# Third modulation in the second mixer, dense layer zero in two phases, and the convolution's first tap on ScalarE

## What is computed

```python
def swiglu(h, wg, wu, wd):
    return (jax.nn.silu(h @ wg) * (h @ wu)) @ wd

def second_block(x, c, ada_w, ada_b, ...):
    cs = jax.nn.silu(c)
    for i in range(2):
        mod = cs @ ada_w[i] + ada_b[i]
        sh1, sc1, g1, sh2, sc2, g2 = [m[:, None, :] for m in jnp.split(mod, 6, axis=-1)]
        h = rms_norm(x, norm_mix_g[i]) * (1 + sc1) + sh1
        if i % 2 == 0:
            mix = hybrid_mixer_2(h, hy_w_in[0], ..., hy_w_out[0], rel_table)
        else:
            mix = conformer_conv(h, cv_w_pw1[0], ..., cv_w_pw2[0], cv_b_pw2[0])
        x = x + g1 * mix
        h = rms_norm(x, norm_ffn_g[i]) * (1 + sc2) + sh2
        x = x + g2 * swiglu(h, ffn_w_gate[i], ffn_w_up[i], ffn_w_down[i])
    return rms_norm(x, final_norm_g)
```

## Time and profile before

| | us |
|---|---|
| median of 3 runs (lowest, highest) | 1461.85 (1460.13, 1463.21) |
| the profiled execution | 1465.13 |
| its span | 1463.4 |
| TensorE busy | 1376.3 (94%) |
| VectorE busy | 870.7 (60%) |
| ScalarE busy | 275.6 (19%) |
| GpSimd busy | 265.6 (18%) |
| mean granted clock | 0.976 |
| DMA | 355.58 MB, 243 GB/s |

### The profile page before, as it was taken

How to read it: one execution, slowest core, us unless ns; L and a number is a source line. 1 busy time by engine, 2 the same in 40 slices (tenths; PEclk the granted TensorE clock), 3 DMA queues, 4 the chain that set the end, 5 groups by cost and what they waited for, 6 DMA issues and landing times. The chain is left out here.

```text
span 1463.4 us, 18944 instructions
## 1 busy us (share of the span) xinstructions
PE 1376.3 (94%) x7517; PEld 1015.5 (69%) x7517; DVE 870.7 (60%) x1464; ACT 275.6 (19%) x602; POOL 265.6 (18%) x342
## 2 busy tenths in 40 slices
PE   5999999896776999999999999999999999999997
PEld 1877655653442788768888888777766878888843
DVE  2458775432232668753454685788783874777864
ACT  2222221000000311643345101000002113211101
POOL 5078010000000300553355402100020100000000
PEclk9999999998888999999999999999999999999999
DMA  9976887899999697866774455898854552555431
GB/s 350 310 263 226 285 329 298 348 417 415 416 418 385 191 305 261 306 194 162 159 180 133 160 162 176 327 333 322 297 210 150 155 156 73 163 168 172 170 129 47
DMA packets 176057, 355.58 MB, mean 243 GB/s; under 512 B 7289, under 2 KB 137041, under 8 KB 158561
## 3 DMA queue, kind: packets, MB, share of 16 engines
q1 hardware_dynamic: 166720, 313.64, 60.4%
q0 software_dynamic: 9248, 40.71, 9.5%
HBM read 352.58 MB, written 1.74 MB: 242 GB/s over the span
## 5 line engine op out<-in xcount | busy, mean ns | idle before, releaser
L1846 PE MATMUL PS<-HT,ring 128*128 128x256 f32 x1152 | 258.3, 382 | 0.1
L1846 PEld LDWEIGHTS PS<-HT,ring 128*128 128x128 f32 x1152 | 215.5, 190 | 36.0 <-issue 7.9
L1542 DVE TENSOR_TENSOR X<-X,PS 128x1024 f32<-128x1024 f32 x14 | 17.1, 1222 | 113.2 <-PE PS L1318 113.2
L1265 PE MATMUL PS<-ring_extra,slot_rows 128*32 128x256 f32 x576 | 56.3, 450 | 27.6 <-DMA ring_extra<-in_expert_w_gate 7.1
L2876 PE MATMUL PS<-HT,ring 128*128 128x256 f32 x352 | 76.8, 379 | 0.0
L2905 PE MATMUL PS<-ada_stage,half_sums 128*128 128x256 f32 x320 | 75.6, 379 | 0.0
L2905 PE MATMUL PS<-ring,half_sums 128*128 128x256 f32 x320 | 75.6, 379 | 0.0
L2876 PEld LDWEIGHTS PS<-HT,ring 128*128 128x128 f32 x352 | 66.7, 190 | 9.0
L2882 PE MATMUL PS<-ring,hid 128*128 128x512 f32 x160 | 71.8, 592 | 0.0
L2905 PE MATMUL PS<-ring,HT 128*128 128x256 f32 x304 | 68.8, 379 | 0.0
L2905 PEld LDWEIGHTS PS<-ring,half_sums 128*128 128x128 f32 x320 | 59.4, 190 | 11.2 <-issue 4.3
(11 more groups left out here) (736 smaller groups left out, 2465.4 us busy)
## 6 DMA issues: line engine op xcount, KB each, us to landing
ring<-in_hy_w_in SPq DMA_DIRECT2D x40, 1024.0 KB, 8.4
ring_extra<-in_w_ada SPq DMA_DIRECT2D x24, 1024.0 KB, 7.9
ada_stage<-in_ada_w POOLq DMA_DIRECT2D x24, 1024.0 KB, 7.3
ring<-in_ffn_w_gate SPq DMA_DIRECT2D x22, 1024.0 KB, 5.9
ring<-in_ffn_w_up SPq DMA_DIRECT2D x22, 1024.0 KB, 5.8
ring<-in_ffn_w_down SPq DMA_DIRECT2D x22, 1024.0 KB, 5.8
ring_extra<-in_expert_w_down SPq DMA_DIRECT2D x18, 1024.0 KB, 22.9
ring_extra<-in_expert_w_up SPq DMA_DIRECT2D x18, 1024.0 KB, 20.1
```

The lines of the kernel that those rows point to most:

```text
L1265: mm = pe.matmul(PS[e * SLOTS:(e + 1) * SLOTS, 2, j * CW:(j + 1) * CW], hs[:, k, e * SLOTS:(e + 1) * SLOTS], w[e][:, k, :], start=(k == 0) ...
L1542: dve.tensor_tensor(part, part, PS[:, 6:8, :], ALU.add).then_inc(added, 1)
L1846: mm = pe.matmul(dst, w[:, k, half * P:(half + 1) * P], HT[:, k, :], start=(k == 0), stop=(k == KT - 1))
```

## The change

1. Dense layer zero takes the form of dense layer one (`SPLIT_ORDER` for both, the functions get the layer f). The weight sums of its first chunk are made by VectorE in the second mixer, between `combine_a(1)` and `combine_b(1)`.
2. The third modulation moves into the second mixer. Its 24 fetches go on SyncE's queue, between the ring's loads, into two buffers in turn (a region of the convolution's and the second modulation's stage); a fetch waits until the add two before it is done. The 24 adds stand at `THIRD_ADDS` on VectorE. TensorE sums at (25, 0), (31, 0) and (36, 3) (4, 2 and 2 matmuls of 512 columns, each after 8, 16, 24 adds) and turns at (25, 2), (31, 2) and (37, 1); ScalarE copies between; VectorE finishes at (25, 3), (31, 3) and (37, 1). `value(m)` waits for the first finish (m < 4) or the second, the output projection for the third. Bias rows are small loads now, added by small operations.
3. At the end of dense layer zero the row sums and columns go; `gate_rows` moves between the two halves of the norm's turning.
4. ScalarE does the first tap of the mixer's convolution (24 operations), VectorE the other three.
5. The second modulation's adds come a step earlier, and the value sums are spread anew.
6. Buffers: `third_acc` is carried from the mixer to the end, other slabs are cut anew, and GpSimd makes `tap_blocks` and loads the second gate's bias only once dense layer zero is done.

```diff
-        add_at = {(s, 3): s - 2 for s in range(2, 18)}
+        ADD_PLACES = [(s, 3) for s in range(1, 14)] + [(14, 2), (15, 1), (16, 0)]
+        add_at = {at: a for a, at in enumerate(ADD_PLACES)}
+        THIRD_ADDS = ((20, 2), (21, 1), (21, 2), (22, 0), (22, 2), (23, 1), (24, 0), (24, 3), (25, 2), (26, 1), (27, 0), (27, 3),
+                      (28, 2), (29, 1), (30, 0), (30, 3), (31, 2), (32, 1), (33, 0), (33, 3), (34, 2), (35, 1), (35, 3), (36, 2))
...
-        v_sum_at = {(14, 3): (0, 0), (15, 1): (0, 1), (15, 2): (0, 2), (15, 3): (0, 3),
-                    (16, 1): (1, 0), (17, 2): (1, 1), (17, 3): (1, 2), (18, 1): (1, 3)}
+        v_sum_at = {(14, 3): (0, 0), (15, 3): (0, 1), (16, 1): (0, 2), (16, 2): (0, 3),
+                    (17, 0): (1, 0), (17, 3): (1, 1), (18, 0): (1, 2), (18, 2): (1, 3)}
...
+                def fetch_third(a):
+                    if a == 0:
+                        sp.wait_ge(used, base + V0 + 3)
+                    elif a == 1:
+                        sp.wait_ge(cols, 1)
+                    else:
+                        sp.wait_ge(third_summed, a - 1)
+                    sp.dma_start(third_stage[a % 2].rearrange("p (a n) -> p a n", a=1), wv3[:, ds(a % KT, 1), a // KT, :])\
+                        .then_inc(third_in[a % 2], 16)
...
                 for s in range(NP + 12):
+                    for a in range(THIRD):
+                        if (THIRD_ADDS[a - 2] if a > 1 else ((19, 1), (20, 1))[a]) in ((s, 0), (s, 1)):
+                            fetch_third(a)
...
                     send_until(sp, base + s + 1)
+                    for a in range(2, THIRD):
+                        if THIRD_ADDS[a - 2] in ((s, 2), (s, 3)):
+                            fetch_third(a)
...
+                    pe.wait_ge(third_made, 2 if m >= 4 else 1)
...
+                def sum_third(c):
+                    pe.wait_ge(third_summed, THIRD_READY[c])
...
+                    for g in range(2 * len(THIRD_PARTS[c])):
+                        v = third_acc[:, THIRD_PARTS[c][g // 2], :].rearrange("p (m h k) -> p h k m", h=2, k=KT // 2)[:, g % 2]
+                        mm = pe.matmul(PS[32 * g:32 * g + 32, 7, :], ones[:, 0:32], v, start=True, stop=True,
+                                       tile_position=(0, 32 * g))
+                    mm.then_inc(third_rowsum, 1)
...
+                def tap(s):
...
+                    act.wait_ge(evac, s + 1)
+                    for m in range(2):
+                        tile = 2 * XORDER[s] + m
+                        act.activation(conv_tiles(s)[:, m, :], RX[:, s % 3, m, 0:S], ACT.Identity, scale=convT[:, tile:tile + 1],
+                                       bias=convT[:, CONV * XT + tile:CONV * XT + tile + 1]).then_inc(first_tap, 1)
...
+                def add_third(a):
+                    g, k = a // KT, a % KT
+                    dve.wait_ge(third_in[a % 2], 16 * (a // 2 + 1))
+                    dst = third_acc[:, THIRD_AT[g]:THIRD_AT[g] + 2, :].rearrange("p a n -> p (a n)")
+                    if k == 0:
+                        dve.tensor_scalar(dst, third_stage[a % 2], cv[:, 0:1], None, ALU.mult).then_inc(third_summed, 1)
+                    else:
+                        dve.wait_ge(third_summed, a)
+                        dve.scalar_tensor_tensor(out=dst, in0=third_stage[a % 2], scalar=cv[:, k:k + 1], in1=dst,
+                                                 op0=ALU.mult, op1=ALU.add).then_inc(third_summed, 1)
...
                 combine_a(1)
+                first_gate, first_up = (segs["ffn0"].base + j for j in range(2))
+                for n in (first_gate, first_up):
+                    dve.wait_ge(landed[slots[n]], 16 * turns[n])
...
                 combine_b(1)
...
     def chunk(f, kind, e):
-        return FFN_BASE[f] + (order, SPLIT_ORDER)[f].index((kind, e))
+        return FFN_BASE[f] + SPLIT_ORDER.index((kind, e))
```

More of the change, by code:

```diff
@@ L2929, in seven @@
                 hs7 = lambda j: [hsum[:, j, k, :] for k in range(4)]
-                ws7 = lambda j: [wsum[:, e % 2, j, k, :] for k in range(4)]
-                arrive(pe, n_g)
-                arrive(pe, n_u)
-                pe.wait_ge(combined, weights_summed(f, e))
-                if e > 1:
-                    pe.wait_ge(combined, row_sum(f, e - 1, 2))
-                product(P2, rows(1, 0), half(gate, 1))
-                product(P1, rows(0, 0), half(gate, 0)).then_inc(used, 1)
-                if e > 1:
-                    pe.wait_ge(combined, row_sum(f, e - 1, 5))
@@ L3007, in split_gate_up @@
-            def split_gate_up(e, norm):
-                n_g, n_u = chunk(1, "g", e), chunk(1, "u", e)
-                gate, up = w_slot(n_g), w_slot(n_u)
-                half = lambda ap, h: [ap[:, 4 * h + k, :] for k in range(4)]
-                rows = lambda h, i: [HT[:, 4 * h + k, i * P:(i + 1) * P] for k in range(4)]
-                hs7 = lambda j: [hsum[:, j, k, :] for k in range(4)]
-                ws7 = lambda j: [wsum[:, (e + 1) % 2, j, k, :] for k in range(4)]
+                ws7 = lambda j: [wsum[(e + 1) % 2][:, j, k, :] for k in range(4)]
@@ L3128, in _ @@
             turn(0)
-            ffn(0, 0, turn_vectors, modulation_rows)
-            modulation_columns()
-            gate_rows(1, 0, 0)
-            pe.wait_ge(gated, 4)
-            turn(1)
+            for e in range(FFN_CHUNKS):
+                split_gate_up(0, e, 0)
+                if e == 0:
+                    turn_vectors()
+            for gi in range(len(DOWN_GROUPS)):
+                split_down(0, gi)
+            whole_down(0)
+            turn_row(1, 0)
+            gate_rows(GATE_MIX, 0)
+            turn_row(1, 1)
             for f in range(KT):
@@ L3412, in split_sum_weights @@
-            def split_sum_weights(e):
-                for n in (chunk(1, "g", e), chunk(1, "u", e)):
-                    dve.wait_ge(landed[slots[n]], 16 * turns[n])
-                if e >= 2:
-                    dve.wait_ge(sevens, PE_MARKS[1, e - 2, "P4"])
-                gate, up = w_slot(chunk(1, "g", e)), w_slot(chunk(1, "u", e))
-                t1, t2, t4 = (wsum[:, (e + 1) % 2, j] for j in range(3))
-                step(dve.tensor_tensor(t1, up[:, 0:4, :], gate[:, 0:4, :], ALU.subtract))
-                step(dve.tensor_tensor(t2, up[:, 4:8, :], t1, ALU.subtract))
-                step(dve.tensor_tensor(up[:, 0:4, :], up[:, 4:8, :], up[:, 0:4, :], ALU.subtract))
-                dve.tensor_tensor(t4, gate[:, 4:8, :], t2, ALU.subtract).then_inc(combined, 1)
```

678 lines of the change are left out of this document (249 added, 429 removed).

## The result

The changed kernel takes 1503.55 us (median of 4 runs, 1503.2 to 1504.75) where the kernel before takes 1461.51 (4 runs): a ratio of 1.0287, with a 95% interval of 1.0272 to 1.0302. It is **42 us slower**. The forecast was slower by 5 us, with 1477 as the upper end of the range. The direction was right; the size was not, and neither were most of the places.

The account below looks back on a forecast made before the run. TensorE was taken to bound the second mixer and dense layer zero. Dense side -11.3, sums and turns +6.3, waits +10.6 gave +5.6, taken as +5.2: 1467 us as a median, range 1456 to 1477.

Parts of the forecast that it names:

- What I cost at nothing: Priced at zero: first tap on ScalarE, 24 fetches on SP's queue, GpSimd's later tap blocks and bias load.
- steps 20 to 23: Mixer, before the first score: five adds delay `move_y(15)`, a TensorE wait of 0.5 to 4 us, taken as 2.2.
- the value stage: Value products, steps 14 to 18: waits vanish or grow with tighter fetches, -1.3 to +2.5 us, taken as +0.5.
- ahead of the first pointwise product: From dense layer zero's end to the first pointwise product: 7.0 us instead of 5.0, a loss of 1.9.
- The gain in dense layer zero: Dense layer zero takes dense layer one's form: 207.6 us instead of 220.8, -13.2, its weight sums hidden on VectorE.
- Sums and turns on TensorE: Mixer: three third-modulation sums (5.0 us) and three turns (1.3) add 6.3 us, bounds 5.3 to 7.3.
- Waits for adds in the attention: TensorE waits for VectorE's adds: 3.0, 2.2 and 1.0 us at the three sums, 1.0 and 0.7 at `value`.
- the 3.09 us each, from which 1470 was worked out: Attention: adds contending with GpSimd take 3.09 us instead of 2.35, four waits grow 0.74 each: 1470 instead of 1467.
- rival 4: TensorE's clock falls after waits of about 3 us, each fall costing 2 to 3 us: 1469 to 1473; chance 0.05.
- Rival 1: VectorE is in time at sums (25,0), (31,0) and their values, so waits vanish: 1456.9 or 1455.5; chance 0.30.
- Rival 2: Transfers bind the attention: bias loads, ring and fetches need 116% of the DMA engines, 1475 to 1482; chance 0.15.
- Rival 3: Dense layer zero misses dense layer one's length: late first chunk or unhidden sums cost 3 to 5 us; chance 0.05.

Follow-up runs that it names:

- mended_shifted: Changed kernel with small loads apart, tap blocks later, value stage's adds and sums as before, and the third modulation's schedule one slot later: 1471.35 us.
- small adds: Changed kernel with small loads apart, tap blocks later, value stage as before, and third-modulation adds cut to 16 of 2048 columns: 1472.88 us.

## Why the prediction was wrong, point by point

The steps that failed are the waits and "What I cost at nothing". Of the +44.6 the sum had +2.2 for steps 20 to 23 (+10.3 measured), nothing for setup (+10.3), +0.5 for the value stage (+7.5), +1.9 ahead of the first pointwise product (+7.5), and for the attention some 11 us, two sums with their turns and four waits, where +19.0 were measured. The gain in dense layer zero held.

**Dense layer zero** and its weight sums: right. 207.74 us against 207.6 forecast, and nothing new ahead of it: 109.76 to its first product, 2.7 more than before, of which the third sum and turn are 2.5.

**To the first pointwise product:** 7.0 forecast, 12.55 measured. The step that failed is "What I cost at nothing". I asked only when GpSimd's tap blocks are needed, not what runs beside them: VectorE's scaling. With that mended the term is 6.4. The Trainium skill ("SBUF — State Buffer", section Who interferes with whom) says that a VectorE operation in a two-port mode, which `tensor_scalar` can enter, and GpSimd lock each other out, and that whoever issues first keeps the ports for the whole instruction. The 7.58 us here agree in kind, but go further: VectorE was held not for one instruction of GpSimd's but through all four (7.54 us together). That GpSimd's products hold it is shown by the edit; that it is through the ports no run here shows.

**Sums and turns on TensorE:** +6.3 forecast. The three sums, in TensorE's timeline of the changed kernel:

```profile
723.62 2.04 PE L2043 MATMUL PS<-third_acc,ones 128*32 128x512 f32 x8 [2.21 <-DVE third_acc L2485]
...
790.92 2.03 PE L2043 MATMUL PS<-third_acc,ones 128*32 128x512 f32 x4 [5.64 <-DVE third_acc L2485]
...
848.77 2.01 PE L2043 MATMUL PS<-third_acc,ones 128*32 128x512 f32 x4
```

Each takes 2.0 us, two groups no less than four, so 6.1, just over my upper bound of 6; with the turns 7.4. The term was mis-sized by 1 us.

**Waits for adds in the attention:** 3.0, 2.2 and 1.0 us were taken for the three sums; 2.2, 5.6 and none were measured. The two at `value` (1.0 and 0.7) are not there. The first sum's is the size that VectorE's order gives; it stays at 2.2 without the fetches. The second takes a late fetch and the adds' own time together: it is 1.2 without the fetches and 1.4 with small adds. The adds ahead of these two sums took 2.34 and 2.61 us, so the 3.09 us each, from which 1470 was worked out, did not come either. What the sum had no term for is the rest of the 19.0 us: after sums, turns (5.0) and waits (8.6), the work itself ran slower, since TensorE's busy time in the attention is 133.3 us, 10.4 more than before, of which the sums are 5.0.

**The clock** (rival 4, chance 0.05) is that remainder: without the fetches, at a granted clock of 1.00, the work beside the sums takes only 0.6 us more than before. Behind the waits of 5.4, 2.2, 10.2, 2.2 and 5.6 us in the mixer and those of 2.6 and 3.9 us behind dense layer zero the granted clock fell to 0.5, the 1.2 GHz level; behind the 1.95 us ahead of dense layer zero, behind 2.8 us in the value stage, and behind 2.2 us at the first sum of the kernel without the fetches, it did not, so the 3 us that I put between the two do not divide them. I priced one fall at 2 to 3 us; the attention's three cost 5.4 together, and setup's alone some 5. I had one wait in mind; there were seven.

**Steps 20 to 23:** 2.2 us taken, 4 as the upper end, 10.2 measured. The row for a fetch's landing came from a stretch without bias loads, and 9.9 was its slowest; fetches here took up to 16.4 us. That was the bound that failed.

**The value stage:** +0.5 taken, 2.5 as the upper end; +7.5 measured: the waits are 5.7 us instead of 1.3, and the rest is the clock. I knew the tighter fetches and took them for half a gain. The experiments put 3.5 us on the packing of the adds and leave the rest open.

**Setup:** no term at all, +10.3 measured. The four small loads were named among what the change adds and not followed to who waits for the last of them. That one semaphore counts all small loads, and TensorE's setup waits for all of them, stands in the code. That they land too late only with a pause of 5.4 us on GpSimd, which goes with the adds' new places, could not be read from it.

**The rivals.** Rival 1 fell at both sums that it names; at their values TensorE indeed waited for nothing. Rival 2, at 0.15, was right in part: the DMA engines' share in the attention rose from 0.67 to 0.85, and adds waited for fetches, 12.6 us ahead of the first score and 4.8 in the attention. The table of stretches, the attention of the kernel before ends at 800.61, so it is compared by these rows of the changed kernel and of mended_shifted:

```profile
700.69:842.59 141.90, 133.26 (x733) 105.97 (x733) 102.96 (x153) 53.51 (x142) 82.52 (x83) 0.94 0.85 251
```

```profile
673.90:817.00 143.10, 134.15 (x735) 105.41 (x734) 103.46 (x153) 53.66 (x142) 76.62 (x83) 0.96 0.90 266
```

Over the 29 us that answer to the earlier trace rows (722.2 to 751.4) the share is 0.94; the 1.16 of the rival's sum was reached only in single stretches of 3 us (773 to 776). Whether the transfers were at their limit there is not shown; but fetches landed late, and a double buffer of 1 MB needs each fetch in time, not the mean. Rival 3 fell.

## What to carry to other kernels

Work moved to an engine that is idle on the average is paid for at every place where that engine stands ahead of the bound one: check, for each moved instruction, what is queued behind it and by when its transfer lands in the stretch it is moved to, not in the one it came from. Follow the smallest added loads to the semaphore that counts them. Ask of each engine that starts earlier or later whom it now runs beside, and where a wait of several microseconds on TensorE is likely, keep a second price for the work behind it at half clock: here that followed seven of nine waits of 1.9 us and more.

## What was not expected of the hardware

- A `tensor_scalar` of 128 x 1024 on VectorE took 7.58 us beside GpSimd's products and 0.75 apart from them.
- Beside VectorE's adds of 128 x 2048, GpSimd's additions of 0.73 us took up to 2.85; the adds themselves 2.35 to 2.96. GpSimd's busy time in the attention rose from 54.6 to 82.5 us, with the same work. The adds make it: 55.6 with small adds, 83.4 without the fetches.
- A sum with a matrix of ones against columns read 32 bytes apart takes 2.0 us for two groups of 512 columns and for four; the one at 790.92 took 2.03 at a granted clock of 0.50, the one at 848.77 2.01 at 1.00.
- Of two waits on TensorE in the value stage, 2.8 us left the granted clock at 1.00 and 2.2 us, eleven microseconds later, brought it to 0.50.
